# Experts of a grouped MoE on one core: empty places left out of the gathers, results returned by an indirect store

## The reference, cut to what matters

```
probs = softmax(xt @ w_router + b_router)          # 16 experts in 4 groups
group = best by the sum of its two best; idx, vals = top 2 in it
comb  = one_hot(experts) * vals / sum(vals)
for e in range(16):
    h = silu(xt @ w_gate[e]) * (xt @ w_up[e])      # 1024 -> 512
    y = y + comb[:, e:e+1] * (h @ w_down[e])       # 512 -> 1024
```

## Time and profile before

| | us |
|---|---|
| median of 3 runs | 1943.31 (1941.78 to 1950.37) |
| the profiled execution's own time | 1937.43 |
| its span | 1935.5 |
| TensorE busy (matmul) | 1524.2 |
| VectorE, ScalarE, GpSimd busy | 734.2, 418.5, 343.8 |

### The profile page before, as it was taken

The page is one execution under the profiler, slowest core; times in us unless marked ns, Lnnn a source line. Parts: engine busy times, 40 slices in busy tenths (PEclk is TensorE's granted clock), DMA queues, the critical chain, the costliest instruction groups (busy, mean ns, idle before and its releaser), DMA issues. The chain is left out here.

```text
span 1935.5 us, 22055 instructions
## 1 busy us (share of the span) xinstructions
PE 1524.2 (79%) x7374; PEld 709.0 (37%) x7375; DVE 734.2 (38%) x1282; ACT 418.5 (22%) x908; POOL 343.8 (18%) x268
## 2 busy tenths in 40 slices
PE   5899986694679998656998887777596599989950
PEld 3333335242333333203466564344343233333320
DVE  1001127675200000075946577995275300000018
ACT  1001013221121222222120002334421021212222
POOL 0000000000100000033735566550000000000004
PEclk8999998596789999967999998888797699999985
DMA  8573614605699999799789999884503499999962
GB/s 314 213 276 119 263 45 152 223 23 198 243 426 427 427 395 428 287 374 332 281 302 403 408 387 407 334 334 177 191 12 141 187 421 410 427 428 427 429 277 89
DMA packets 123149, 563.05 MB, mean 291 GB/s; under 512 B 13685, under 2 KB 43238, under 8 KB 101419
## 3 DMA queue, kind: packets, MB, share of 16 engines
q1 hardware_dynamic: 94530, 492.46, 63.9%
q10 hardware_dynamic: 19584, 37.28, 5.1%
q0 software_dynamic: 8944, 32.15, 4.4%
HBM read 521.82 MB, written 40.03 MB: 290 GB/s over the span
## 5 line engine op out<-in xcount | busy, mean ns | idle before, releaser
L1571 PE MATMUL ps<-arena_w,arena_r 128*64 128x512 f32 x1600 | 363.9, 611 | 32.4 <-issue 27.5
L1571 PEld LDWEIGHTS ps<-arena_w,arena_r 128*64 128x64 f32 x1600 | 121.8, 141 | 268.3 <-issue 262.1
L1553 PE MATMUL ps<-arena_w,arena_r 128*64 128x512 f32 x800 | 180.0, 597 | 19.4 <-ACT arena_r L1601 19.4
L1648 DVE TENSOR_TENSOR arena_r<-arena_r,ps 128x512 f32<-128x512 f32 x38 | 26.1, 688 | 425.9 <-ACT arena_r L1618 425.9
L1954 POOL TENSOR_TENSOR arena_w<-arena_w,arena_r 128x1024 f32<-128x1024 f32 x48 | 115.8, 2417 | 106.4 <-DMA arena_w<-in_cache_k_dram 105.9
L1954 POOL TENSOR_TENSOR arena_r<-arena_r 128x1024 f32<-128x1024 f32 x48 | 115.7, 2416 | 51.3 <-DMA arena_r<-in_cache_k_dram 51.2
L2007 PE MATMUL ps<-arena_w,xt 128*128 128x256 f32 x512 | 123.4, 402 | 1.4 <-ACT xt L2180 1.4
L449 PE MATMUL ps<-arena_w,xt 128*128 128x512 f32 x256 | 114.0, 601 | 1.0 <-DVE arena_w L530 0.6
L1069 PE MATMUL ps<-arena_w,xt 128*128 128x512 f32 x256 | 111.4, 593 | 0.0
L2007 PEld LDWEIGHTS ps<-arena_w,xt 128*128 128x128 f32 x512 | 102.4, 203 | 17.9 <-ACT xt L2180 1.5
L1503 POOL COPY small<-idx 128x1 int32 (+1 forms) x38 | 7.0, 183 | 520.9 <-PE ps L1519 456.3
(11 more groups left out here) (382 smaller groups left out, 1926.1 us busy)
## 6 DMA issues: line engine op xcount, KB each, us to landing
arena_w<-in_w_exp_gate_dram SPq DMA_DIRECT2D x38, 2048.0 KB, 16.9
arena_w<-in_w_exp_up_dram SPq DMA_DIRECT2D x38, 2048.0 KB, 21.8
arena_w<-in_w_exp_down_dram SPq DMA_DIRECT2D x38, 2048.0 KB, 18.4
arena_m<-in_cache_v_dram SPq DMA_DIRECT2D x128, 512.0 KB, 7.4
arena_w<-in_cache_k_dram SPq DMA_DIRECT2D x64, 512.0 KB, 9.7
arena_r<-in_cache_k_dram SPq DMA_DIRECT2D x64, 512.0 KB, 9.1
arena_w<-in_w_ada_dram SPq DMA_DIRECT2D x12, 2048.0 KB, 20.5
arena_m<-in_w_ada_dram SPq DMA_DIRECT2D x12, 2048.0 KB, 9.3
```

The costliest lines, as they stand in the source:

```text
L1553: last = nc.tensor.matmul(psy[c][at:at + 64, :], ht[u][:, k, 64 * (1 - a):64 * (2 - a)], wd[u][:, k, c * 512:(c + 1) * 512], start=(k == 0 ...
L1571: last = nc.tensor.matmul(ps[at:at + 64, :], xgt[u][:, k, 64 * a:64 * (a + 1)], w[u][:, k, :], start=(k == 0), stop=(k == KT - 1), tile_po ...
```

## The change

- In the experts, the gather gets a bound (`bounds_check=TOK - 1`, not an error if exceeded): a place whose index is over 519 is left out, and what the buffer held before stays there. The route stage gives every empty place the index 8192 (`NOWHERE`): it subtracts 8192 from the token numbers ahead of the one-hot matmuls and adds it back in the copy of the sum.
- The result's store moves from ScalarE's queue (a direct DMA) to GpSimd (an indirect DMA, `scatter`). Its index list `m.spot` is the slot's own number, plus 8192 at an empty place, and slots over 3071 are left out. In a step GpSimd issues the gather of tile n, then waits for both result copies of tile n-4, copies its column of `m.spot`, drains and issues the store; the last four stores come after the loop.
- The route stage fills two buffers of the gathered rows (2048 columns) with zeros on GpSimd, makes one table more there, and VectorE has three small operations more with two drains.
- The fill of layer 0 covers all 24 tiles (12288 KB, before 4096 KB). Three of the four parts of the states are loaded ahead of it, the fourth after its landing.

```diff
+            def scatter(u, n):
+                g.wait_ge(y_v, n + 1)
+                g.wait_ge(y_s, n + 1)
+                nc.gpsimd.tensor_copy(spc[u], m.spot[:, bass.ds(n, 1)])
+                g.drain()
+                g.indirect_dma_start(out=m.yD, out_offset=bass.IndirectOffsetOnAxis(ap=spc[u], axis=0), in_=ys[u], in_offset=None,
+                                     bounds_check=SLOTS - 1, oob_is_err=False).then_inc(y_out[u], 16)
...
                 g.indirect_dma_start(out=xg[u], out_offset=None, in_=m.xmD,
-                                     in_offset=bass.IndirectOffsetOnAxis(ap=ixc[u], axis=0)).then_inc(x_in[u], 16)
+                                     in_offset=bass.IndirectOffsetOnAxis(ap=ixc[u], axis=0),
+                                     bounds_check=TOK - 1, oob_is_err=False).then_inc(x_in[u], 16)
+                if t is None or t == LAST:
+                    scatter(u, 2 * i + u - 4)
             pairs = tiles(g, step)
+            for j in range(4):
+                scatter(j % 2, 2 * pairs - 4 + j)
...
-                s.wait_ge(y_s, n + 1)
-                s.wait_ge(y_v, n + 1)
-                s.dma_start(m.yD[bass.ds(n * P, P), :], ys[u]).then_inc(y_out[u], 16)
...
+            nc.gpsimd.iota(spot, pattern=[[P, SLOT_TILES]], base=0, channel_multiplier=1,
+                           allow_small_or_imprecise_dtypes=True).then_inc(tab, 1)
+            nc.gpsimd.memset(m.R[:, 0:2 * D], 0.0)
...
+            V.tensor_scalar(tok, tok, -float(NOWHERE), None, ALU.add)
+            v.drain()
             tt(tok, tok, valid, ALU.mult)
...
-            V.tensor_copy(m.idx[:, :], m.ps[4][:, 0:SLOT_TILES])
+            V.tensor_scalar(m.idx[:, :], m.ps[4][:, 0:SLOT_TILES], float(NOWHERE), None, ALU.add)
+            V.tensor_scalar(vacant, m.ps[4][:, 0:SLOT_TILES], 0.0, float(NOWHERE), ALU.is_equal, ALU.mult)
+            v.drain()
+            V.tensor_tensor(m.spot[:, :], vacant, spot, ALU.add)
...
-            most = 2 * MIN_PAIRS * P
-            sp.dma_start(m.yD[most:SLOTS, :].rearrange("(t p) n -> p t n", p=P),
-                         m.lnr[:, 0:1, :].to_broadcast([P, (SLOTS - most) // P, D])).then_inc(y_fill, 16)
+            for n in range(3):
+                states.load(sp, n)
+            sp.dma_start(m.yD.rearrange("(t p) n -> p t n", p=P),
+                         m.lnr[:, 0:1, :].to_broadcast([P, SLOT_TILES, D])).then_inc(y_fill, 16)
             sp.wait_ge(y_fill, 16)
-            for n in range(NS // 2):
-                states.load(sp, n)
+            states.load(sp, 3)
```

More of the change, by code:

```diff
@@ L36 @@
 MIN_PAIRS = NE // 2
+NOWHERE = 8192
 LAST = SLOT_TILES + 1
@@ L86, in allocate @@
     m.idx = sb("idx", [P, SLOT_TILES], I32)
+    m.spot = sb("spot", [P, SLOT_TILES], I32)
     m.texp = sb("texp", [1, SLOT_TILES + 1], I32)
@@ L1219, in stage_route @@
     slot, row = take(2, NTT), take(1, NJ)[:, 0, :]
+    spot, vacant = take(1, SLOT_TILES)[:, 0, :], take(1, SLOT_TILES)[:, 0, :]
     reached, token_at, row_hot = take(NJ, SLOT_TILES + 1), take(NJ, SLOT_TILES), take(NJ, P)
@@ L1267, in _ @@
             pe.wait_ge(sel_ok, 1)
-            pe.wait_ge(tab, 11)
+            pe.wait_ge(tab, 12)
             nc.tensor.matmul(m.ps[3][:, 0:NTT * NE], m.ones[:, :], before[:, :, 0:NTT].rearrange("p e i -> p i e"),
@@ L1334, in _ @@
             tt(gs, gs, g3, ALU.max)
-            v.wait_ge(tab, 11)
+            v.wait_ge(tab, 12)
             def first_of(onehot, score, best, weights, n):
@@ L1469, in stage_experts @@
     ixc = [m.small[:, 504 + u:505 + u].bitcast(I32) for u in range(2)]
+    spc = [m.small[:, 506 + u:507 + u].bitcast(I32) for u in range(2)]
     pst = [m.ps[0], m.ps[1]]
```

## The result

The changed kernel takes 1984.08 us in the median of 3 runs (1980.69 to 1987.93), against 1943.31 before: a ratio of 1.0218, 95% interval 1.0184 to 1.0251. It is slower by 41 us. The forecast was 1938.3, with a range up to 1951.

A forecast was written before the change was run, and what follows sets the result against it. In the expert stages TensorE and DMA were both taken to be at their limit. -11 (stages) + 4.8 (stage ends) + 1.1 (route) = -5 from 1937.4 gave 1932.3, median 5.9 higher: 1938.3; own range 1930 to 1950, stated range 1915 to 1951.

The forecast's parts named there:

- the store's new path within the loop: Expert loop: store hidden, result copies wait for the store two steps before; four more GpSimd instructions, some 2 us a tile.
- isn't held: GpSimd in the expert loop: waiting for tile n-4's copies doesn't delay tile n+1's gather, which needs step n-2's transposes.
- Rival 3: Expert loop: stores taking over 23 us to land hold result copies and TensorE; 1968 at 24 us, chance 0.09.
- Stages, -11: Both expert stages: shorter weight waits from fewer row bytes, 5.3 plus 8.7, together 14, taken as 11, ends 3 and 14.
- The bunching of the filled rows: Expert transfers: four-neighbour blocks leave the busiest engine 124 of 144 and 118 of 160 rows; 0.34 and 0.65 us a tile saved.
- The waits predicted to remain: Ahead of gate and up products: 13 to 20 us left over both layers, less gone in layer 0 than layer 1.
- The end of a stage, +2.4 a layer: Last result copy to combine's gather: later by about 1.0 + 1.4 us, 4.8 for two layers, bounds 2 to 10.
- Route, +0.55 a layer: Route stage: small VectorE operations and drains on the path, 1.1 us in all, bounds 0.5 and 2; GpSimd zeros cost nothing.
- Fill, nothing: Layer 0's larger fill: lands by 327, before the queue's wait for the prompt's state ends at 333.69; costs nothing.
- Rival 2: Expert transfers: skipping saves no transfer time; gain 0 to 3, costs 6, giving 1948; chance 0.15.
- rival 1: Expert transfers: rows go round all DMA engines, -30 + 6 = -24, giving 1919; chance 0.27.
- The sum -5: Whole kernel: stages -11, ends of stages +4.8 and route +1.1 together.

The follow-up runs named there:

- e1: Changed kernel with the drain between each index copy and its indirect DMA replaced by a semaphore and a small GpSimd addition: 1940.16 us, ratio to before 0.9984.
- e5: Kernel before plus an end stage of 2 MB indirect gathers, with different rows left out, then with drains or semaphores: six full gathers took 34.2 us.
- e8: Changed kernel with the drain ahead of the gather kept and only the one ahead of the store replaced by a semaphore: 1933.12 us, ratio 0.9931.
- e6: e1 with no place left out, so gather and store move all 128 rows: 1951.11 us, ratio to before 1.0041.
- e10: e1 with neighbouring ranks put on different DMA engines, no drain, timed on one chip with e11: 1929.89 us, ratio to before 0.9924.
- e11: Repeat of e1 (both drains replaced by semaphores) on the chip of e12: 1940.11 us, ratio to before 0.9984.
- e9: Changed kernel with rows spread over DMA engines, drain kept ahead of the gather, semaphore ahead of the store: 1923.21 us, ratio to before 0.9891.
- e12: Repeat of e8 (drain ahead of the gather only) on the chip of e11: 1930.65 us, ratio to before 0.9934.
- e4: Kernel before with only the new fill of all 24 tiles and the change's order of state loads: 1944.21 us, ratio 1.0011.

## Why the prediction was wrong

**The step that failed** is the store's new path within the loop: "GpSimd holds four more instructions a tile, some 2 us of a 12 to 20 us step", and so nothing waits. It took the gap of 0.84 us between index copy and gather in the earlier trace rows for the drain's price. The drain has no price of its own: it lasts until the indirect DMA ahead of it has landed. In the kernel before that was one landing a tile of 4.0 to 13.2 us, mostly hidden behind the wait for the transposes. The change put a second one into every tile, so GpSimd's loop became two landings long, about 23 to 25 us where both were slow (552.10, 576.99, 601.08, 624.18 for four gathers in a row), for steps that take TensorE 12.7 us (half) to 23. The bound moved to GpSimd's queue: the gather of tile n+1 stood behind the drain of the store of tile n-4. The landings of the single DMAs in the changed kernel, e1, e5 and e8 show it from four sides.

**The claim that the gather "isn't held"** followed the semaphores only (it needs TensorE's step n-2) and forgot that what is queued behind a drain waits for what the drain waits for.

**Rival 3** had the sign (1968, chance 0.09) and the place, GpSimd's queue and the result copies, which did wait for stores in the end (159.8 us on VectorE). Its mechanism was not what happened: it wanted stores that take over 23 us to land, and they landed in 12.2 at most; VectorE waited because the stores were issued late, behind a drain.

**Stages, -11: borne out with the drains gone.** e6 against e1 gives 11 us for the skipping; in the changed kernel itself it can't be seen. The bunching of the filled rows, taken at 0.49 against 0.27 for an even spread, is shown by e5, and the rows spread by hand (e10 against e11, e9 against e12) give back 7 to 10 us of what it had cost. The Trainium skill (DMA: Bandwidth & Descriptors, section The descriptor swizzle) gives the map for a transfer to 128 partitions and doesn't speak of indirect ones; the four series agree with it for an indirect gather too, 33.0 us with rows 64 to 127 left out against 34.2 with all. The waits predicted to remain, 13 to 20 us over both layers, were 7.8 in the changed kernel, where rows were late and not weights, and 20.4 in e1, a little over the range. There, as said, less went in layer 0 (15.6 to 14.5) than in layer 1 (11.9 to 5.8), but the slow products behind them didn't shrink (6.8 and 4.4 us, before 6.5 and 3.1).

**The end of a stage, +2.4 a layer: too small without the drain.** From the last result copy to combine's gather it was 4.10 us before and 5.5 in the changed kernel, 1.4 more; with one drain (e12) 6.1, with none (e11) 8.5, which is 4.4 more a layer.

**Route, +0.55 a layer: near** (0.6 in layer 0, -0.2 in layer 1). **Fill, nothing: right** (e4). **Rival 2** (skipping saves nothing) falls with e6, **rival 1** (an even spread) with e5.

The sum -5 leaves the drains out, and e1 is the run that has none: 1940.16 where before took 1942.8, so -3. Of that, the skipping gave 11 and the new path took some 7 (e6 against before), where -11 and +5.9 had been put down. It is not the kernel of the forecast, though, which has its drains.

## What to carry to other kernels

Before adding a DMA to an engine's queue, read that queue's own timeline from the first tile on, gap by gap, and ask of each instruction that has a gap what its longest one means; a short gap late in a loop can be a long wait that is covered. A drain on GpSimd beside indirect DMAs is a wait for their landing: between an index copy and its DMA a semaphore does the same with half a microsecond of idle time. Try both, though: here one drain a tile, ahead of the gather, was better than none. And bytes left out count only on the DMA engine that is the last to finish: with the filled rows at one end of a tile, half the bytes took nearly the whole time (e5), and another order of the rows gave 7 to 10 us.

## What the runs showed of the hardware

- A drain on GpSimd waits for indirect DMAs in flight: 9.6 to 10.7 us between 2 MB gathers that otherwise start 1.3 us apart (e5), and in the loop of the changed kernel the DMA behind it starts 0.83 to 0.90 us after the landing, 67 times out of 67, for landings of 2.6 to 12.2 us.
- An indirect DMA of 128 rows is split over the DMA engines by the position of the row, in blocks of four neighbours and apart for the two halves of 64: six gathers took 34.2 us with all rows, 33.0 with rows 64 to 127 left out, 33.1 with the second four of each eight left out, and 19.8 with the odd rows left out (e5).
- Places left out still leave a packet. The queue of GpSimd's DMAs (packets, MB, share) in e6, where all rows are moved, and in e1, where the empty places are left out:

```profile
q0 software_dynamic: 14416, 52.08, 6.9%
```

```profile
q0 software_dynamic: 14416, 29.29, 4.2%
```

  The packets are the same to the last one, while 22.79 MB are gone, which is 5564 rows of 4 KB. Such packets cost little: with every other row left out, on all engines alike, six gathers took 19.8 us, 2.7 over half of the 34.2 of full ones (e5).
- The fastest kernel here leaves empty places out both ways, spreads the rows over the DMA engines and keeps one drain (e9): 1923.21 us, 0.9891 of the kernel before and 0.97 of the changed one (1923.21 / 1984.08, timed apart).
